# Dots of gathered rows spread over the retrieval heads, with four row buffers and keys loaded per head

## The reference

```
def peer(a, w_q, k1, k2, u_exp, v_exp):
    q = (a @ w_q).reshape(B, S, PEER_HEADS, PEER_QDIM)
    s1 = jnp.einsum('bshd,hnd->bshn', q[..., :half], k1)
    s2 = jnp.einsum('bshd,hnd->bshn', q[..., half:], k2)
    t1, i1 = lax.top_k(s1, PEER_TOPK)
    t2, i2 = lax.top_k(s2, PEER_TOPK)
    cand = t1[..., :, None] + t2[..., None, :]          # 256 a head
    cand_idx = i1[..., :, None] * PEER_KEYS + i2[..., None, :]
    top, sel = lax.top_k(cand, PEER_TOPK)
    experts = jnp.take_along_axis(cand_idx, sel, axis=-1)
    gates = jax.nn.softmax(top, axis=-1)
    h = jnp.einsum('bthkd,btd->bthk', u_exp[experts], a)
    w = gates * gelu(h)
    return jnp.einsum('bthk,bthkd->btd', w, v_exp[experts])
```

## Time and profile before

| | us |
|---|---|
| median of 3 runs | 3241.17 |
| lowest and highest of them | 3237.96, 3245.41 |
| the profiled execution | 3231.75 |
| its span, first to last instruction | 3229.9 |

### The profile page before, as it was taken

One profiled execution on the slowest core, in us unless ns is written; L12 is line 12 of the kernel. 1 busy time (PEld: TensorE's weight loads), 2 busy tenths in 40 slices (PEclk: granted clock), 3 DMA queues, 4 the chain that ended last, 5 costly groups with the idle time before them and its releaser, 6 DMA issues.

```text
span 3229.9 us, 42906 instructions
## 1 busy us (share of the span) xinstructions
PE 3125.2 (97%) x16812; PEld 2932.2 (91%) x16812; DVE 2189.7 (68%) x3013; ACT 1002.6 (31%) x1036; POOL 1304.1 (40%) x687
## 2 busy tenths in 40 slices
PE   8999999999999995999999998999999999999998
PEld 6888678899999995999899998999999999999887
DVE  5565653566666664667666788788888888887545
ACT  5234432332233331222222232323323222233422
POOL 1010000028888888878787323333333233330000
PEclk9999999999999997999999999999999999999999
DMA  8472213245555555999999889888888888885322
GB/s 304 142 251 92 79 66 104 92 135 135 134 129 130 130 135 160 331 307 333 300 323 325 352 342 355 319 311 331 311 312 315 315 328 308 319 310 194 104 102 91
DMA packets 209414, 739.19 MB, mean 229 GB/s; under 512 B 71953, under 2 KB 125201, under 8 KB 132993
## 3 DMA queue, kind: packets, MB, share of 16 engines
q1 hardware_dynamic: 90768, 409.55, 34.9%
q0 software_dynamic: 100080, 302.69, 29.1%
q10 hardware_dynamic: 18432, 25.17, 2.2%
HBM read 682.60 MB, written 54.72 MB: 228 GB/s over the span
## 4 chain that ended last, share of the span: by engine, by line
PE 63%; POOL 27%; issue 5%; DMA 2%; DVE 2%; ACT 0%; SPq 0%; DVEq 0%; ACTq 0%; POOLq 0%
POOL gates L442 23%; PE ps L1489 20%; PE ps L1490 20%; PE ps L1491 20%; POOL rows_u L459 4%; DMA gates<-gates_r,idx_d 1%; PE ps L1662 1%; PE ps L1681 1%; PE ps L1661 0%; DVE wL L819 0%; DMA raw<-s_v 0%; DMA rows_v<-u_rows,idx_s 0%; DVE ssum L831 0%; DMA rows_u<-u_rows,idx_s 0%; DVE hT L1458 0%
## 5 line engine op out<-in xcount | busy, mean ns | idle before, releaser
L1489 PE MATMUL ps<-aH,wH 128*128 128x384 f32 (+2 forms) x3088 | 1091.5, 353 | 61.9 <-DVE wL L819 59.8
L1490 PE MATMUL ps<-aL,wH 128*128 128x384 f32 (+2 forms) x3088 | 1085.6, 352 | 0.0
L1491 PE MATMUL ps<-aH,wL 128*128 128x384 f32 (+2 forms) x3088 | 1085.5, 352 | 0.0
L476 ACT ACTIVATE wH<-raw 128x2048 fp32r<-128x2048 f32 x333 | 637.9, 1916 | 1050.7 <-PE ps L1491 976.7
L442 POOL DMA_INDIRECT gates<-gates_r,idx_d x384 | 758.0, 1974 | 397.8 <-DVE gates_r L1211 255.5
L819 DVE TENSOR_TENSOR wL<-raw,wH 128x2048 fp32r<-128x2048 f32 x333 | 761.7, 2287 | 230.2 <-ACT wH L476 229.0
L1489 PE MATMUL ps<-actH,wH 128*128 128x384 f32 x2048 | 685.3, 335 | 9.0 <-DVE wL L819 6.3
L1490 PE MATMUL ps<-actL,wH 128*128 128x384 f32 x2048 | 684.8, 334 | 0.0
L1491 PE MATMUL ps<-actH,wL 128*128 128x384 f32 x2048 | 684.8, 334 | 0.0
L1489 PEld LDWEIGHTS ps<-aH,wH 128*128 128x128 f32 x3088 | 582.5, 189 | 107.3 <-DVE wL L819 66.0
L1490 PEld LDWEIGHTS ps<-aL,wH 128*128 128x128 f32 x3088 | 582.7, 189 | 38.4 <-issue 1.0
(11 more groups left out here) (244 smaller groups left out, 1812.3 us busy)
## 6 DMA issues: line engine op xcount, KB each, us to landing
raw<-s_pu SPq DMA_DIRECT2D x128, 1024.0 KB
raw<-s_pv SPq DMA_DIRECT2D x128, 1024.0 KB
gates<-zeros POOLq DMA_DIRECT2D x24, 1024.0 KB, 8.6
pre<-ut ACTq DMA_DIRECT2D x128, 192.0 KB
pre_in<-pre SPq DMA_DIRECT2D x128, 192.0 KB
gate_in<-gates SPq DMA_DIRECT2D x128, 192.0 KB
raw<-s_out SPq DMA_DIRECT2D x16, 1024.0 KB
raw<-s_pq SPq DMA_DIRECT2D x16, 1024.0 KB
```

The costliest lines, as they stand in the source:

```text
L476: A(wH[parity][:, :], raw[parity][:, :], ACT.Copy).then_inc(hi_ready, 1)
L1489: mm(out, wh, xh, start=start, stop=False)
L1490: mm(out, wh, xl, start=False, stop=False)
L1491: return mm(out, wl, xh, start=False, stop=stop)
```

## The change

- **Transposes early.** The 16 transposes of the last 128 tokens stand in head 0, behind its first tile, in banks 2, 3, 6 and 7. ACT's copies and DVE's `a_tok` follow there too.
- **Dots in the heads.** DVE does 5 dots in each of the heads 1 to 7, at fixed places between the top-k steps: 35 (`EARLY`). The other 93 are spread evenly over the chunks 50 to 117 (`dot_at`). None is left for the second matrix, and ACT's gelu of the dots moves to chunk 124.
- **POOL.** From `routed` of head 0 on it issues gather 0, gather 1 and 7 adds, and then a gather and 7 adds each time, until gather 35, which waits for the last routing. Behind it the adds are 2, 2, 1 again.
- **Row buffers.** The first 35 rows use two buffers, the rest of the first matrix four, and the second matrix four others, behind the last chunk. Row j waits for the dot that last used its buffer.
- **Added rows.** 6 in group 0, from slot 2 on, and 122 spread over the 112 slots of groups 1 to 14 (`add_at`).
- **Keys.** SP loads the keys of one head at a time (128 KB) into two buffers. From head 2 on it waits until the scores of head h - 2 are done.
- DVE's and SP's loops over the heads, and DVE's over the chunks, are written out. Some small tiles of the top-k work lie at other places.

```diff
+FORTH = [2, 3, 6, 7]
+HEAD_DOTS = 5
+EARLY = HEAD_DOTS * (HEADS - 1)
 FIRST_DOT = ROUTE_U + 2
-LOOP_DOTS = 3 * ((KEYS - FIRST_DOT) // 2)
-GROUP_PICKS = 9
-HEADS_FIRST = 5
+LAST_DOT = KEYS - GROUP - 2
+def dot_at(c):
+    return EARLY + (min(max(c, FIRST_DOT), LAST_DOT) - FIRST_DOT) * (PICKS - EARLY) // (LAST_DOT - FIRST_DOT)
+def add_at(g, q):
+    first = 6
+    if g == 0:
+        return max(0, q - 2)
+    return first + (GROUP * (g - 1) + q) * (PICKS - first) // (GROUP * (NGROUPS - 2))
+for _j in range(2 * PICKS):
+    _at = _j % 2 if _j < EARLY else _j % 4 + (4 if _j >= PICKS else 0)
+    ROW_USED.append(max([j for j in range(_j) if ROW_AT[j] == _at], default=-1))
...
@@ load_head (SP), behind the two query tiles @@
+                if h >= 2:
+                    sp.wait_ge(ps_done, 2 * h - 2)
+                else:
+                    sp.wait_ge(act_lo, N_SC["ffn"])
+                sp.dma_start(keys[h % 2][:, :, :], a["keys"][:, h, :, :]).then_inc(keys_loaded[h % 2], 16)
...
@@ gpsimd @@
-            added = HEADS_FIRST * NTD * TOPK
-            for n in range(added):
-                add_gates(n)
+            added = 0
             pool.wait_ge(a_tok_ready, 1)
             for j in range(2 * PICKS):
-                if j >= 3:
-                    pool.wait_ge(pick_done, j - 2)
-                if j == LOOP_DOTS:
+                if j < PICKS and j % TOPK == 0:
+                    pool.wait_ge(routed, j // TOPK + 1)
+                if j == EARLY:
+                    pool.wait_ge(routed, HEADS)
+                if j == PICKS:
                     pool.wait_ge(tile_done, CUM[S0["pv"] - 1])
+                if ROW_USED[j] >= 0:
+                    pool.wait_ge(pick_done, ROW_USED[j] + 1)
...
-                for n in range(added, min(added + (1 if j % 3 == 2 else 2), HEADS * NTD * TOPK)):
-                    add_gates(n)
-                    added = n + 1
+                if j >= 1:
+                    for n in range(added, min(added + (7 if j <= EARLY else 2 - (j % 3 == 2)), HEADS * NTD * TOPK)):
+                        add_gates(n)
+                        added = n + 1
...
@@ retrieve (DVE) @@
                     index_of(0)
+                    if h >= 2:
+                        dot(j0)
                 lo(n + 2, 0)
...
                     route_head(h - 1)
+                    if h >= 2:
+                        dot(j0 + 1)
...
                 pair_maxima(h)
+                if h == 1:
+                    dot(j0)
...
                 pair_more(h)
+                if h == 1:
+                    dot(j0 + 1)
+                if not first:
+                    dot(j0 + 2)
                 scale_chunk(uc + 4, 0, CUM[n + 6])
+                if not first:
+                    dot(j0 + 3)
                 lo(n + 8, 0)
                 pair_indices(h)
+                if not first:
+                    dot(j0 + 4)
...
@@ the chunks behind the heads (DVE) @@
+            for c in range(FIRST_DOT, KEYS):
+                scale_chunk(c - 1, (c - 1) % 2, CUM[nu + c - 1])
+                for j in range(dot_at(c), dot_at(c + 1)):
+                    if j == dot_at(c) + 1:
+                        lo(nu + c + 1, (c + 1) % 2)
+                    dot(j)
+                if dot_at(c + 1) - dot_at(c) < 2:
+                    lo(nu + c + 1, (c + 1) % 2)
```

More of the change, by code:

```diff
@@ L152, in trunk_layer @@
     pqT = [at(f"pqT{i}", [2, T], F, W0 + 4 * KB * i) for i in range(2)]
-    keys = at("keys", [HEADS, 2, KEYS], F, W0 + 8 * KB)
+    keys = [at(f"keys{i}", [2, KEYS], F, M0 + (12 + i) * KB) for i in range(2)]
     ACT_AT = [W0, W0 + 24 * KB]
@@ L156, in trunk_layer @@
     actL = [at(f"actL{i}", [GROUP, TD], R, ACT_AT[i] + 12 * KB) for i in range(2)]
[L157 to L158 removed]
+    rows = [at(f"rows{i}", [D], F, W0 + (16 + 8 * i) * KB) for i in range(4)] + \
+           [at(f"rows{4 + i}", [D], F, A0 + 8 * i * KB) for i in range(4)]
     gain_row = at("gain_row", [D], F, W0 + 24 * KB)
[L160 removed]
+    a_tok = at("a_tok", [KD, P], F, W0 + 8 * KB)
     pRaw = at("pRaw", [2, T], F, W0)
@@ L253, in trunk_layer @@
         g_scaled = sem("g_scaled")
-        keys_loaded = sem("keys_loaded")
+        keys_loaded = [sem(f"keys_loaded{i}") for i in range(2)]
         pq_copied, ps_done, tops_done, gate_sub, gate_exp, routed = (
@@ L326, in load_head @@
                     load(n + s, stream["pq"][2 * h + s, :, :], s)
+                if h >= 2:
[3 more added lines that the diff above has]
+                sp.dma_start(keys[h % 2][:, :, :], a["keys"][:, h, :, :]).then_inc(keys_loaded[h % 2], 16)
                 for s in range(HEAD_U):
                     load(n + 2 + s, stream["pu"][HEAD_U * h + s, :, :], s % 2)
-            with sp.Fori(0, HEADS) as h:
+            for h in range(HEADS):
                 load_head(h)
@@ L680, in head @@
                     root("ffn")
+                    for r in range(4):
+                        act.wait_ge(tok_done_h, r + 1)
+                        A(hT[:, 4 * r:4 * r + 4, TD:T], ps[:, FORTH[r], :].rearrange("p (a b) -> p a b", a=4),
+                          ACT.Copy).then_inc(tok_copied, 1)
                 else:
@@ L716, in _ @@
             gate_exps(HEADS - 1)
-            for r in range(4):
-                act.wait_ge(tok_done_h, r + 1)
-                A(hT[:, 4 * r:4 * r + 4, TD:T], ps[:, r, :].rearrange("p (a b) -> p a b", a=4), ACT.Copy).then_inc(tok_copied, 1)
             u_beat(ROUTE_U + 1, 1, nu + ROUTE_U + 1, 0)
@@ L725, in _ @@
                 u_beat(c, c % 2, nu + c, 0)
+                if c == KEYS - 4:
+                    act.wait_ge(pick_done, PICKS)
+                    A(dots[:, :], dots[:, :], ACT.Gelu_apprx_tanh).then_inc(dots_gelu, 1)
                 weight_hi(c - KEYS + GROUP, c - KEYS + GROUP, 0, pre_in[c % 2])
@@ L739, in _ @@
                 v_beat(0, q, 0, nv, 0)
-                if q == GROUP - 2:
-                    act.wait_ge(pick_done, PICKS)
-                    A(dots[:, :], dots[:, :], ACT.Gelu_apprx_tanh).then_inc(dots_gelu, 1)
             for i in range((NGROUPS - 2) // 2):
@@ new lines, in _ @@
+            V.tensor_tensor(pick_w[:, :], dots[:, :], gates_r[:, NTD, :], ALU.mult).then_inc(pick_weighed, 1)
+            dve.wait_ge(pick_weighed, 1)
+            for g in range(NGROUPS - 1):
+                m = nv + GROUP * g
+                for q in range(GROUP):
+                    if (g, q) != (0, 0):
+                        v_begin(g, q, m, 0)
+                    for c in range(add_at(g, q), add_at(g, q + 1)):
+                        if c == add_at(g, q) + 1:
+                            v_low(g, q)
+                        add_row(c)
+                    if add_at(g, q + 1) - add_at(g, q) < 2:
+                        v_low(g, q)
+                    v_end(g, q, g % 2, m, 0)
@@ L1742, in head_slots @@
                     tile(n + s, s, s, waits=N_SC["ffn"] if first and s == 0 else None)
-                    if first:
-                        norm_sum("ffn", 4) if s == 0 else token_rms(NORMS["ffn"] + 1, 5)
+                    if first and s == 0:
+                        norm_sum("ffn", 4)
+                        for k in range(KD):
+                            ins = nc.tensor.transpose(ps[:, FORTH[k // 4], (k % 4) * P:(k % 4 + 1) * P], hT[:, k, TD:T],
+                                                      ident[:, :])
+                            if k % 4 == 3:
+                                ins.then_inc(tok_done_h, 1)
+                    elif first:
+                        token_rms(NORMS["ffn"] + 1, 5)
                 scores(h, b, 0)
```

163 lines of the change are left out of this document (54 added, 109 removed).

## The result

| | before | after |
|---|---|---|
| median, us | 3239.57 (4 runs) | 3280.67 (4 runs) |
| lowest and highest | 3237.95, 3245.41 | 3280.26, 3281.49 |
| the profiled execution | 3231.75 | 3281.49 |
| its span | 3229.9 | 3279.7 |

The ratio is 1.0124, with a 95% interval of 1.0106 to 1.0141. The forecast was 3301 us, range 3255 to 3338. The two profiled executions are 49.7 us apart, where the sum had said 60; the medians are 41.1 us apart, since the profiled execution of before was a quick one.

What follows compares the result with a forecast made beforehand. POOL, issuing gathers and adds and held by DVE's two-operand operations, was taken as the engine behind PE's stall. Stage end +70.8, second matrix -12.4, clock +2 made +60 us on 3241: 3301 us, range 3255 to 3338.

Steps and rivals of the forecast that it cites:

- Gather 34: Heads: POOL's gather 34 starts at 1318.8 us, where PE alone would want dot 34 at about 1199.
- gather 2 starts: Heads: with two buffers gather 2 waits for dot 0, behind head 1's pair maxima, and starts at 744.6 us.
- waits for adds: Heads, gather 2 to gather 34: POOL waits four times for adds to land, 3.6 us each, 14.4 us.
- holds by splits and matches: Heads: DVE's weight splits and index matches of 6.4 heads hold POOL's instructions for 77.5 us.
- holds by 32 dots: Heads: 32 dots on DVE hold POOL's instructions for 0.83 us each, 26.6 us.
- the sign that was named: Heads 2 to 7: PE idles about 16 us in each while DVE's dots wait for rows.
- From gather 34 to the last chunk: Last dot of the heads to last chunk: 79 chunks, 657.3 us, plus 20 of stalls; the last ends at 2007.2.
- The margin behind the heads: First matrix behind the heads: POOL keeps up, 5.91 us a gather with adds against one dot per 6.08 us.
- The second matrix: Start of the second matrix: the 9.0 us of idle time and the clock's 3% go, -12.4 us.
- The small edits: Key loads on SP's queue, ACT's copies and DVE's token operation in head 0: they cost nothing.
- POOL is not held: Rival, heads: adds at 1.85 and gathers at 1.29 us, gather 34 at 1214.7, result 3197 us; chance 0.06.
- The waits take the holds' place: Rival, heads: DVE waiting holds nobody, 16.1 us a gather, gather 34 at 1260, time near 3241; chance 0.06.

Runs made afterwards that it cites:

- e1: The changed kernel without its 384 gate adds and the wait for them, all gathers and dots left in place; 3167.44 us, ratio to before 0.9784.
- e3: The changed kernel with 17 adds instead of 7 behind gather 1 and 6 instead of 7 behind gathers 2 to 11; 3268.21 us, ratio to before 1.0097.
- e2: The changed kernel with each dot replaced by a plain sum of the gathered row, one SBUF operand instead of two; 3263.59 us, ratio to before 1.0082.
- e4: The changed kernel with four dots a head instead of five, ten adds behind gather 1 and eight behind gathers 2 to 28; 3240.91 us, ratio to before 1.0013.
- e5: The changed kernel with gathers, dots, adds and row buffers in before's order, so only the side edits remain; 3235.5 us, ratio to before 0.9991.
- e9: e6 with PE's loop over heads written out and 226 adds instead of 230 ahead of the gathers; 3169.3 us, ratio to before 0.9781.
- e6: e5 with 97 dots instead of 117 in the first matrix, 31 in the second, 230 adds first, gather 0 before the last routing; 3173.73 us, ratio 0.9794.
- e10: e9 with gather 0 behind 216 adds instead of 226, eight adds before gather 1, then two behind every gather; 3167.01 us, ratio to before 0.9764.

## Why the prediction was right

**The bound.** POOL behind DVE behind PE, read from three views of before, was the right chain: e1 takes away POOL's adds and leaves all of DVE's work and all rows, and the stall goes; e3 moves adds into POOL's idle time and wins about that time.

**Gather 34** was forecast for 1318.8 and came at 1308.63. Term by term:

| term | forecast | measured |
|---|---|---|
| gather 2 starts | 744.6 | 743.96 |
| 32 gathers, 224 adds undisturbed | 455.7 | 455.7 (taken over) |
| waits for adds | 14.4 | 9.4 |
| holds by splits and matches | 77.5 | 79.3 (left in e2) |
| holds by 32 dots | 26.6 (0.83 each) | 20.3 (gone in e2) |
| sum | 574.2 | 564.7 |

The 10.2 us by which the forecast is too long are 0.6 of gather 2, 5.0 of waits and 4.5 of holds. The waits were 2.2 to 2.6 us each; the forecast took over the 3.6 of before's heads, 14.4 us in four. The holds come near in sum, and that is partly luck. By the changed kernel's own timeline (see e2) the forecast had the splits, matches and pair sums too high, 77.5 against 60.7, and the dots too low, 26.6 against 39.4. It took 1.51 us a split from a stretch without dots, and 0.83 for a dot from the mean of the earlier trace rows. Put down one by one, the 85 dots of that stretch held POOL by 84.0 us (0.99 each) and the 57 splits by 32.7 (0.57 each): all 57 splits there follow right behind a dot, so the POOL instruction that the dot had held is followed by one that starts late in the split, and that one is held for 0.34 to 0.95 us. What an operation costs POOL depends on where in it the next POOL instruction starts, so it can't be carried over as a price of its own.

**The pace.** Heads 2 to 7 take (1316.6 - 785.2) / 6 = 88.6 us each, forecast 89.7. That is 15.1 us over PE's own 73.5, forecast 16.2, with the slower clock in it, as the forecast said, and not on top. So the sign that was named, PE idle for about 16 us in each of these heads, reads lower: its gaps are 9 to 14 us a head, 11.3 in the mean, and the slower clock is the rest. POOL had the 0.3 us gaps that were named as the sign, and chunks are 8.32 us apart from 1400 on.

**From gather 34 to the last chunk:** 688.4 forecast (1318.8 to 2007.2), 688.5 measured. Within it, gather 35 was forecast 22.7 us behind gather 34 and came 22.5 behind (it waited 6.07 us for the last routing), and dot 36 waited 12.35 us for its row. From chunk 49 to the last it took 666.5 us, of which 649.0 are undisturbed; the forecast had 79 chunks and 20 us.

**The margin behind the heads** of 6.08 against 5.91 us a gather held, but by less than forecast: PE loses 2.4 us from 1400 to 1937, and POOL issues its last add at 1847.94, some 90 us before the end of chunk 120 (1997.11 - 7 x 8.32 = 1938.9), where the gates are first read. POOL grouped by line from gather 35 to the last add (1331 to 1855 us), against the earlier trace rows:

```profile
L468 POOL DMA_INDIRECT gates<-gates_r,idx_d x146 | 310.8, 2129 | 60.0 <-issue 43.6 <-DMA gates<-gates_r,idx_d 16.4
L484 POOL DMA_INDIRECT rows<-u_rows,idx_s x87 | 127.7, 1467 | 32.3 <-issue 26.2 <-DVE gates_r L1236 6.1
```

524 us for 87 gathers with 1.68 adds each are 6.02 us a gather, against 6.08 that a gather may take. e4 shows how thin that is.

**The second matrix** gave back 10.9 us, 12.4 forecast: the idle time of 9.0 us was all there, the rest that was counted for the clock only in part. **The small edits** cost nothing, as forecast, but not for the reason given: in e5 the heads end 11.7 us later, 9.5 of it by PE's pauses and the clock behind them, and it is POOL that hides that. The forecast looked at each edit's instructions and not at what the rewriting would do to PE's loop. In a version in which POOL is not the bound, the pause is paid, at least in part: without it e9 is 4.4 us below e6, and e10, with the adds moved as well, 6.7.

**The rivals.** "POOL is not held" would have needed gather 34 at 1215. "The waits take the holds' place" would have shown a pace near 16 us a gather; it was 564.7 / 32 = 17.6. DVE did wait 132.5 us, in which it holds nobody, but the number of splits and dots per head is the same and each still holds. The third rival did not come in the changed kernel and did in e4.

**On the sum:** 60.7 - 10.9 = 49.8 on the spans; 70.8 - 12.4 + 2 = 60.4 forecast. The 9.4 us by which the median of before lies above its profiled execution did not carry over in full, as all runs of after lie within 1.2 us of the profiled one. That makes the other 9.7 us between 3301 and 3281, which is in no term.
